# Strassen's scheme for two row tile pairs of the merge gates, with later x loads and transposes

## The chip, the cores and the metric
The kernel runs on one core of one Trainium2 chip. The metric is device time in microseconds (us) of one execution, the median of several runs. TensorE (PE) multiplies, VectorE (DVE) and ScalarE (ACT) work elementwise, GpSimd (POOL) does a few elementwise steps, and SyncE (SP) issues the DMAs.

## The reference
One layer of a decoder trunk on x of 256 tokens by 2048 channels, float32. Cut to what matters here:

```
proj = rms_norm(x) @ w_in                       # 2048 x 9216; the last 4096 columns are gate_a | gate_b
y_a = multiscale_pool(u_pool) @ w_branch_a      # 1024 x 2048
y_b = hgrn2(q, f, i, g) @ w_branch_b            # 1024 x 2048
x  += (sigmoid(gate_a) * y_a + sigmoid(gate_b) * y_b) @ w_out
x  += (silu(conv3(u)_gate) * conv3(u)_val) @ w_down,   u = rms_norm(x) @ w_up
x  += sigmoid(rms_norm(x) @ w_ple_gate) * (p @ w_ple)
return rms_norm(x)
```

## The kernel before, in words
Every product is float32 made of three products of split operands. An operand t is cut into t_hi (a rounded copy) and t_lo = t - t_hi, and t times w is t_hi w_hi + t_hi w_lo + t_lo w_hi. So one row tile (128 rows of w, 128 tokens, 512 columns) costs three matmuls (L623 to L625; in the down stage `triple`, L671 to L673).

**Units and slots.** All weights come as a stream of numbered units. A unit is two row tiles of a weight by 512 columns, 512 KB. It passes through a ring of four buffers: SP loads `raw` (`rows`, L464), ACT rounds it into `w_hi` (`split_hi`, L1010), DVE subtracts to get `w_lo` (`split_lo`, L1303), and TensorE runs 12 matmuls on it (two row tiles, two token blocks, three matmuls each) and counts it in `units_done`. ACT and DVE run one list of steps, `slot(s)`, for s = 0, 1, 2 and so on. A slot first splits unit s + 3 (LEAD = 3); everything else that has its time in that slot comes behind it. Because the ring has four buffers, `split_hi(u)` waits for `units_done` of unit u - 4:

```
def split_hi(u, it=None):
    ...
    if u >= RING:
        ac.wait_ge(units_done, plus(u - RING + 1, 2 * UK, it))
```

So slot s of ACT starts when TensorE has finished unit s - 1, and slot s of DVE starts one rounding step later. SP's `slot_split(u)` waits until `w_lo` of unit u - 4 is made, and for a unit of a Strassen pair also for the sums of its weights (L457).

**Stages.** Ten chunks of 8 units are the projections (MIX = 80 units), beside which the scan and the pooling run. The merge stage follows: for each of four column chunks n (512 columns), 8 units of gate a, 8 of gate b, 4 of w_branch_a (y_a) and 4 of w_branch_b (y_b), 24 units in all, each product in one of two halves of the PSUM tensor `main` by turns. ACT applies the sigmoid when a gate is done (`store`), DVE multiplies y_a and y_b with the sigmoids (L1665) and adds the two into `m_tok` (L1670); TensorE transposes `m_tok` into the PSUM tensor `aux` behind the first unit of the next chunk (side job `mT`, L789), and ACT and DVE split the result for w_out (L1213, L1673). Then come w_out (32 units), w_up (176 units), w_down (172 units), and the last gate. `merge_slot(n, k)` is the slot after which chunk n's product k (gate a, gate b, y_a, y_b) is complete.

**The Strassen pairs of the down stage.** Two adjacent column chunks share the activations. At five places of each half (`SEVEN_AT`) a 2 by 2 block problem (two row tiles, two token blocks, two column chunks) is done with 7 products in place of 8. DVE makes four sums of the raw weights (`weight_diffs`, L1548 to L1552) in the slot two ahead, ACT rounds them (L1165), DVE makes their low parts (L1576), and POOL and DVE make sums of the activations (L1842, L1559 to L1571). TensorE runs 3 of the 7 products with the two units and the other 4 in two halves behind the next two units (`down_sums`). Four of the products collect in banks of their own. At the end of each half ACT copies the first (L1184) and DVE combines them (`combine`, L1590), from slot `down_slot(2p) - 4` on, five units after the last pair's first unit; TensorE waits for the fifth combining step, which is in slot `down_slot(2p) - 2`, at the start of the next half, ten units after that pair's first unit.

`x_tok`, the token major x that w_out's result is added to, is loaded in four pieces of 512 KB during the projections (`X_TOK_AT`, L498).

Of the kernel before, what the change touches and what calls it, by code (L numbers as in the profile page):

```python
# [36 lines left out]
P = 128  # L37
# [60 lines left out]
def merge_slot(n, k):  # L98

    return MIX + n * 2 * (UK + UB) + (UK, 2 * UK, 2 * UK + UB, 2 * (UK + UB))[k]  # L100
# [21 lines left out]
SEVENS = [down_unit(p, i) for p in range(2) for i in SEVEN_AT[p]]  # L122
SEVEN = {u: q for q, u in enumerate(SEVENS)}
SUMS_AT = {max(u - 4, DOWN + UK): q for q, u in enumerate(SEVENS)}
N_SEVEN = [len(SEVEN_AT[0]), len(SEVENS)]

# [9 lines left out]
def chunk_end(c):  # L136
# [17 lines left out]
X_TOK_AT = [20, 24, 28, 32]  # L154
# [15 lines left out]
    + [(merge_slot(n, 3) + 1, f"mT{n}") for n in range(NQ)]  # L170
# [21 lines left out]
X2_AT = {down_slot(n) + 2: n for n in range(NQ)}  # L192
COMBINE_AT = [down_slot(2 * p) - 4 for p in range(2)]
# [18 lines left out]
def build(nc, x, x_t, p_t, vecs, convs, w_in, pool_mix_w, w_branch_a, w_branch_b, w_out, w_up, w_down,  # L212
          w_ple_gate, w_ple, ln_final_w, ident_c, levels_c, counts_c, out):
    with ExitStack() as ctx:
# [21 lines left out]
        sb("fill", [P, FILL])  # L236
        x_tok = sb("x_tok", [P, TB, D])
# [124 lines left out]
        x2_turned, copied, combined = map(sem, ("x2_turned", "copied", "combined"))  # L362

# [23 lines left out]
        def main_acc(c, tb, width=NCOL):  # L387
            return main[:, c % 2, tb, 0:width]

# [60 lines left out]
        def _(sp):  # L450
# [43 lines left out]
            for u in range(UK, MIX):  # L494
                rows(u, w_in_v, 2 * (u % UK), PROJ[u // UK])
                if u in X_TOK_AT:
                    n = X_TOK_AT.index(u)
                    sp.dma_start(x_tok[:, :, cols(n)], x_v[:, :, cols(n)]).then_inc(tok_in, 16)  # L498
                if u == 14:
                    sp.dma_start(convT[:], convs).then_inc(conv_in, 16)  # L500
                    sp.dma_start(levels[:], levels_c).then_inc(late_in, 16)
                    sp.dma_start(counts[:], counts_c).then_inc(late_in, 16)
                    sp.dma_start(mixw[:].rearrange("p g a n -> p (g a) n"),
                                 pool_mix_w[0].rearrange("g (a p) n -> p (g a) n", p=P)).then_inc(late_in, 16)
            u = MIX
            for n in range(NQ):
                for w, k, col in ((w_in_v, UK, COL_GA), (w_in_v, UK, COL_GB), (w_a_v, UB, 0), (w_b_v, UB, 0)):
# [53 lines left out]
        def _(pe):  # L561
            def main_released(c):

                if c < 8:
                    g, k = c // 4, c % 4
                    pe.wait_ge((tok_ready, tok_ready, v_ready, g_ready)[k], (4 * g + 2, 4 * g + 4, 2 * g + 2, 2 * g + 2)[k])
                elif c < C_MIX:
                    pe.wait_ge(tok_ready, 8 + 2 * (c - 7))
                elif c < C_WOUT:
                    n, k = (c - C_MIX) // 4, (c - C_MIX) % 4  # L570
                    pe.wait_ge(gates_ready if k < 2 else gated, 4 * n + 2 * (k % 2 + 1))
                elif c < C_UP:
                    pe.wait_ge(x_new, 2 * (c - C_WOUT + 1))
                elif c < C_DOWN:
                    pe.wait_ge(z_read, c - C_UP + 2)
                elif c < C_GATE:
                    pe.wait_ge(combined, 13)
                else:
                    pe.wait_ge((sig_ready, emb_ready)[(c - C_GATE) % 2], 2 * ((c - C_GATE) // 2 + 1))

            def aux_released(name):

                kind, g = name.rstrip("0123456789."), name.split(".")[0][-1:]
                g = int(g) if g.isdigit() else 0
                if kind == "ms":
                    pe.wait_ge(ms_ready, 1)
                elif kind == "qT":
                    pe.wait_ge(qT_ready, g + 1)
                elif kind == "fT":
                    pe.wait_ge(sig_f, 2 * (g + 1))  # L590
                elif kind == "diag":
                    pe.wait_ge(sc_ready, 8 * g + 1)
                elif kind == "prod" and name[-1] != "8":
                    pe.wait_ge(sc_ready, 8 * g + 1 + int(name[-1]))
                elif kind == "prod":
                    pe.wait_ge(scX_ready, g + 1)
                elif kind == "pv":
                    pe.wait_ge(o_ready, g + 1)
                elif kind == "obT":
                    pe.wait_ge(obT_ready, 4 * (g + 1))  # L600
                elif kind == "uT":
                    pe.wait_ge(uT_ready, g + 1)
                elif kind == "mix":
                    pe.wait_ge(yaT_ready, 4 * (g + 1))
                elif kind == "mT":
                    pe.wait_ge(mT_ready, g + 1)
# [53 lines left out]
            def chunk_unit(u, c, i, n, hi, lo, k, **more):  # L660
# [3 lines left out]
                for name in AUX_AT.get(u, ()):  # L664
                    side(name)
                if u in X2_AT:
                    turn_x2(X2_AT[u])

# [15 lines left out]
            def sum_tile(t):  # L684
                return w_sums_hi[:, t, :], w_sums_lo[:, t, :]
# [11 lines left out]
            def down_seven(u, p, i, a):  # L697
# [12 lines left out]
                else:  # L710
                    pe.wait_ge(a_sums_ready, q + 1)
# [3 lines left out]
            def down_sums(u, p, i, half):  # L715
# [4 lines left out]
                if half == 0:  # L720
                    triple(product(p, 1), *act_sum(q, 3), *sum_tile(0), start=first, stop=end)
                    mm = triple(product(p, 3), *act_sum(q, 1), *sum_tile(1), start=first, stop=end)
                else:
                    triple(product(p, 2), *act_sum(q, 0), *sum_tile(2), start=first, stop=end)
                    mm = triple(down_acc(2 * p, 1), *act_block(2 * i + 1, 1), *sum_tile(3), start=False, stop=False)
# [57 lines left out]
            def transposes(name, src, n=4):  # L783

                dst = aux_blocks(name)
                for b in range(n):
                    for tb in range(TB):
                        at = in_time(tb) if name[:2] in ("mT", "uT") else slice(tb * P, (tb + 1) * P)
# [57 lines left out]
            def side(name):  # L846
# [25 lines left out]
                elif name[:2] == "mT":  # L872
                    pe.wait_ge(m_ready, int(name[2]) + 1)
                    transposes(name, tok_block(m_tok))
# [32 lines left out]
            for n in range(NQ):  # L907
                for k, (hi, lo, nu) in enumerate(((xT_hi, xT_lo, UK), (xT_hi, xT_lo, UK),
                                                  (yaT_hi, yaT_lo, UB), (obT_hi, obT_lo, UB))):
                    for i in range(nu):  # L910
                        if n == 0 and i == 0 and k >= 2:

                            pe.wait_ge((yaT_ready, obT_ready)[k - 2], 8)
                        chunk_unit(u, C_MIX + 4 * n + k, i, nu, hi, lo, 2 * i)
# [21 lines left out]
            for p in range(2):  # L936
                if p:
                    pe.wait_ge(combined, 5)
# [59 lines left out]
        def _(ac):  # L998
# [153 lines left out]
            def sums_hi(q, part):  # L1152

                if part == 0:
                    ac.wait_ge(a_summed, q + 1)
                    if q > 1:
                        ac.wait_ge(w_sums_done, 2 * (q - 1))
                    ac.activation(a_sums_hi[:, q % 2].rearrange("p k t -> p (k t)"), a_sums[:].rearrange("p k t -> p (k t)"),
                                  ACT.Copy).then_inc(a_sums_hi_ready, 1)
                else:  # L1160
# [4 lines left out]
                    ac.activation(w_sums_hi[:, 2 * half:2 * half + 2, :], w_sums[:, 2 * half:2 * half + 2, :],  # L1165
                                  ACT.Copy).then_inc(w_sums_hi_ready, 1)

            def slot(s):
# [9 lines left out]
                if s in SEVEN:  # L1178
                    sums_hi(SEVEN[s], 2)
                for p in range(2):  # L1180
# [21 lines left out]
                for n in range(NQ):  # L1202
                    if s == merge_slot(n, 0):
                        if n:
                            ac.wait_ge(m_ready, n)
                        else:
                            ac.wait_ge(dT_ready, 2)
                        store(C_MIX + 4 * n, lambda tb: sig_a[:, tb, :], 0, gates_ready, ACT.Sigmoid)
                    if s == merge_slot(n, 1):
                        store(C_MIX + 4 * n + 1, lambda tb: sig_b[:, tb, :], 0, gates_ready, ACT.Sigmoid)  # L1210
                    if s == merge_slot(n, 3) + 2:
                        aux_arrived(ac, f"mT{n}")
                        ac.activation(mT_hi[:, 4 * n:4 * n + 4, :], aux_blocks(f"mT{n}"), ACT.Copy).then_inc(mT_hi_ready, 1)  # L1213
# [78 lines left out]
        def _(dve):  # L1292
# [274 lines left out]
            def sums_lo(q, part):  # L1567
# [5 lines left out]
                else:  # L1573
                    half = slice(2 * (part - 1), 2 * part)
                    dve.wait_ge(w_sums_hi_ready, 2 * q + part)
                    dve.tensor_tensor(w_sums_lo[:, half, :], w_sums[:, half, :], w_sums_hi[:, half, :].bitcast(F32),  # L1576
                                      ALU.subtract).then_inc(w_sums_ready, 1)

            combines = [0]

            def combine(p, part):
# [10 lines left out]
                if part == 0:  # L1592
                    dve.wait_ge(copied, p + 1)
# [15 lines left out]
            def slot(s):  # L1609
# [11 lines left out]
                for k in range(2):  # L1621
                    if s - k in SEVEN:
                        sums_lo(SEVEN[s - k], k + 1)
                for p in range(2):
# [34 lines left out]
                for n in range(NQ):  # L1659
# [6 lines left out]
                    if s == merge_slot(n, 3):  # L1666
                        dve.wait_ge(gated, 4 * n + 4)
                        if n:
                            aux_arrived(dve, f"mT{n - 1}")
                        dve.tensor_tensor(m_tok[:], sig_a[:], sig_b[:], ALU.add).then_inc(m_ready, 1)  # L1670
                    if s == merge_slot(n, 3) + 2:
                        dve.wait_ge(mT_hi_ready, n + 1)
                        dve.tensor_tensor(mT_lo[:, 4 * n:4 * n + 4, :], aux_blocks(f"mT{n}"),  # L1673
# [118 lines left out]
        def _(pool):  # L1792
# [42 lines left out]
            def join_act(u, q):  # L1835

                k = u - DOWN - 2 * UD * (u >= DOWN + 2 * UD)
                if q == 0:
                    pool.wait_ge(aT_ready, NUP)
                else:  # L1840
                    pool.wait_ge(a_sums_ready, q)
                pool.tensor_tensor(a_sums[:], aT_hi[:, k:k + 2, :].bitcast(F32), aT_lo[:, k:k + 2, :].bitcast(F32),  # L1842
# [6 lines left out]

            root(1)  # L1850
# [3 lines left out]
            for q, u in enumerate(SEVENS):  # L1854
                join_act(u, q)
# [51 lines left out]
```

## Time and profile before

| | us |
|---|---|
| median of 3 runs | 1436.45 (1436.11 to 1436.77) |
| the profiled execution: own time | 1436.71 |
| the profiled execution: span from first to last instruction | 1434.9 |
| TensorE busy in the span | 1424.6 (99%) |
| DVE busy | 990.4 (69%) |
| ACT busy | 761.5 (53%) |
| POOL busy | 168.8 (12%) |
| mean granted TensorE clock | 0.999 |

A matmul's entry lasts longer than its turn on the engine, since matmuls are pipelined; what one costs is the distance between two starts.

### The profile page before, as it was taken

How to read it: one execution, taken by the hardware profiler on the slowest of the kernel's cores; microseconds unless marked ns; L12 is line 12 of the kernel's file. 1: busy time of each engine (PE TensorE's matmuls, PEld its weight loads, DVE VectorE, ACT ScalarE, POOL GpSimd, SP SyncE). 2: the span in 40 equal slices, each digit the busy share in tenths (PEclk: the TensorE clock that was granted, in tenths of full speed). 3: DMA queues.
4: the chain of work that ended last, by engine and by line, in shares of the span. 5: the costliest groups of instructions: out<-in, count | busy, mean ns of one | idle time of the engine just before them, and what ended most of it. 6: DMA issues, size and time to landing. Idle time of an engine off the chain costs nothing.

```text
span 1434.9 us, 19704 instructions
## 1 busy us (share of the span) xinstructions
PE 1424.6 (99%) x7112; PEld 1211.5 (84%) x7112; DVE 990.4 (69%) x1220; ACT 761.5 (53%) x920; POOL 168.8 (12%) x113
## 2 busy tenths in 40 slices
PE   9999999999999999999999999999999999999997
PEld 7888888888888888888888888888888888888886
DVE  7676777845455455566777777777777888887755
ACT  7555655544444444555555555555555555555644
POOL 0044144100000000000101101111011100000000
PEclk9999999999999999999999999999999999999999
DMA  9765555556666655465666566565665665556653
GB/s 326 224 205 161 163 174 164 155 183 191 191 190 191 191 191 189 157 207 183 188 191 191 179 198 185 182 200 178 192 192 175 204 205 192 175 192 220 228 199 123
DMA packets 190876, 273.47 MB, mean 191 GB/s; under 512 B 11744, under 2 KB 103136, under 8 KB 190688
## 3 DMA queue, kind: packets, MB, share of 16 engines
q1 hardware_dynamic: 190384, 272.30, 59.9%
q8 instruction: 38, 0.62, 0.2%
q10 hardware_dynamic: 432, 0.37, 0.1%
q14 instruction: 22, 0.18, 0.0%
HBM read 270.53 MB, written 2.10 MB: 190 GB/s over the span
## 4 chain that ended last, share of the span: by engine, by line
PE 98%; DVE 1%; issue 0%; DMA 0%; ACT 0%; ACTq 0%; POOLq 0%; POOL 0%; DVEq 0%
PE main L623 15%; PE main L624 15%; PE main L625 15%; PE aux L748 11%; PE main L748 11%; PE aux L757 6%; PE main L757 6%; PE aux L671 3%; PE aux L672 3%; PE aux L673 3%; PE main L671 3%; PE main L673 3%; PE main L672 2%; PE aux L819 1%; PE aux L789 1%; PE aux L842 0%
## 5 line engine op out<-in xcount | busy, mean ns | idle before, releaser
L1303 DVE TENSOR_TENSOR w_lo<-raw,w_hi 128x1024 fp32r<-128x1024 f32 (+1 forms) x490 | 604.3, 1243 | 387.6 <-ACT w_hi L1010 387.1
L1010 ACT ACTIVATE w_hi<-raw 128x1024 fp32r<-128x1024 f32 (+1 forms) x490 | 515.0, 1052 | 547.2 <-PE main L625 282.6
L623 PE MATMUL main<-w_hi,xT 128*128 128x512 f32 x702 | 276.7, 394 | 0.3 <-DVE w_lo L1730 0.3
L625 PE MATMUL main<-w_hi,xT 128*128 128x512 f32 x702 | 273.6, 390 | 0.0
L624 PE MATMUL main<-w_lo,xT 128*128 128x512 f32 x702 | 273.5, 390 | 0.0
L748 PE MATMUL aux<-xT,w_hi 128*128 128x512 f32 x704 | 169.8, 391 | 0.0
L748 PE MATMUL main<-xT,w_hi 128*128 128x512 f32 x672 | 163.0, 391 | 0.0
L623 PEld LDWEIGHTS main<-w_hi,xT 128*128 128x128 f32 x702 | 132.0, 188 | 27.3 <-DVE xT L1330 1.0
L625 PEld LDWEIGHTS main<-w_hi,xT 128*128 128x128 f32 x702 | 131.8, 188 | 27.4
L624 PEld LDWEIGHTS main<-w_lo,xT 128*128 128x128 f32 x702 | 132.0, 188 | 26.1
L748 PEld LDWEIGHTS aux<-xT,w_hi 128*128 128x128 f32 x704 | 129.4, 188 | 25.2 <-issue 0.3
L748 PEld LDWEIGHTS main<-xT,w_hi 128*128 128x128 f32 x672 | 123.3, 188 | 23.5
L1848 POOL TENSOR_TENSOR act<-cv 128x512 f32<-128x512 f32 (+1 forms) x22 | 71.9, 3266 | 418.9 <-DVE cv L1527 418.9
L757 PEld LDWEIGHTS aux<-xT,w_lo 128*128 128x128 f32 x704 | 90.3, 191 | 3.4
L757 PE MATMUL aux<-xT,w_lo 128*128 128x256 f32 x704 | 91.3, 283 | 0.0
L757 PEld LDWEIGHTS main<-xT,w_lo 128*128 128x128 f32 x672 | 86.4, 191 | 3.4
L757 PE MATMUL main<-xT,w_lo 128*128 128x256 f32 x672 | 87.5, 283 | 0.0
L1527 DVE SCALAR_TENSOR_TENSOR cv<-z,convT,cv 128x255 f32<-128x255 f32 (+1 forms) x172 | 71.7, 479 | 3.0
L1795 POOL TENSOR_TENSOR st<-st,minus_half 128x2 f32<-128x2 f32 (+1 forms) x5 | 3.2, 642 | 530.6 <-DVE st L1361 399.6
L1141 ACT ACTIVATE cv<-z,convT 128x256 f32<-128x256 f32 x86 | 44.8, 591 | 24.1 <-DVE z L1518 24.1
L671 PE MATMUL aux<-w_hi,aT_hi 128*128 128x512 f32 x142 | 55.6, 391 | 0.0
L671 PE MATMUL main<-w_hi,aT_hi 128*128 128x512 f32 x142 | 55.4, 390 | 0.0
(270 smaller groups left out, 1737.3 us busy)
## 6 DMA issues: line engine op xcount, KB each, us to landing
raw<-in_w_up SPq DMA_DIRECT2D x336, 256.0 KB
raw<-in_w_in SPq DMA_DIRECT2D x136, 512.0 KB
raw<-in_w_down SPq DMA_DIRECT2D x84, 512.0 KB
raw<-in_w_out SPq DMA_DIRECT2D x32, 512.0 KB
raw<-in_w_ple_gate SPq DMA_DIRECT2D x32, 512.0 KB
raw<-in_w_branch_a SPq DMA_DIRECT2D x16, 512.0 KB
raw<-in_w_branch_b SPq DMA_DIRECT2D x16, 512.0 KB
raw<-in_w_in SPq DMA_DIRECT2D x15, 256.0 KB, 5.6
```

What stands on the lines that cost most here:

```text
L623: pe.matmul(acc, th, wh, start=first, stop=False)
L624: pe.matmul(acc, th, wl, start=False, stop=False)
L625: return pe.matmul(acc, tl, wh, start=False, stop=end)
L671: pe.matmul(acc, th, wh, start=start, stop=False)
L672: pe.matmul(acc, th, wl, start=False, stop=False)
L673: return pe.matmul(acc, tl, wh, start=False, stop=stop)
L748: mm = pe.matmul(up_acc(j, b), w_hi[:, u % RING, a, b * P:(b + 1) * P], xT[:, k, :, :].rearrange("p h t -> p (h t)"), start=(k == 0), stop ...
L757: mm = pe.matmul(up_acc(j, b)[:, 0:SEQ], w_lo[:, u % RING, a, b * P:(b + 1) * P], xT[:, k, 0, :], start=False, stop=False)
L1010: ac.activation(w_hi[:, u % RING, :, 0:w], raw[:, u % RING, :, 0:w], ACT.Copy).then_inc(hi_full, 1)
L1303: dve.tensor_tensor(w_lo[:, u % RING, :, 0:w], raw[:, u % RING, :, 0:w], w_hi[:, u % RING, :, 0:w].bitcast(F32), ALU.subtract).then_inc(lo ...
L1527: last_op = dve.scalar_tensor_tensor(out=cv[:, b, d:SEQ], in0=z[:, b, 0:SEQ - d], scalar=convT[:, tap, f0(f)], in1=cv[:, b, d:SEQ], op0=AL ...
L1848: pool.tensor_tensor(act[:, 0:nf, :], cv[:, 0:nf, :], cv[:, nf:2 * nf, :], ALU.mult).then_inc(prod_u, 1)
```

## The change
For merge chunks 1 to 3 the units of gate a and gate b alternate, one row tile pair i of both at a time (`gate_unit(n, i, a)`), and both gates add up in `main`, a in half 0 and b in half 1. At i = 2 and i = 5 (`GATES_AT`) the pair is done with 7 products in place of 8. Four of these collect in `aux`. y_a and y_b of every chunk now use `aux` as well. ACT copies one of the products, DVE combines the four (`combine_gates`) and adds the combined terms to both gates (`sum_gates`), and ACT applies the sigmoids in place. The activation sums are made once, during chunk 0, and serve all three chunks. Their weight sums lie in new tensors at the address of `x_tok`; `x_tok` is therefore loaded later, during y_a and y_b of chunk 3, behind a wait of SP for the last weight sums. The transposes of `m_tok` move from behind the first to behind the third unit of the next chunk, always into `aux[0]`. In the down stage only counters change.

```diff
 def merge_slot(n, k):
-    return MIX + n * 2 * (UK + UB) + (UK, 2 * UK, 2 * UK + UB, 2 * (UK + UB))[k]
+    return MIX + n * 2 * (UK + UB) + (2 * UK - 1 if n and k == 0 else UK, 2 * UK, 2 * UK + UB, 2 * (UK + UB))[k]
+def gate_unit(n, i, a=0):
+    return MIX + n * 2 * (UK + UB) + 2 * i + a
...
+GATES_AT = (2, 5)
+N_GATES = len(GATES_AT) * (NQ - 1)
+SEVENS = [gate_unit(n, i) for n in range(1, NQ) for i in GATES_AT] + [down_unit(p, i) for p in range(2) for i in SEVEN_AT[p]]
...
-X_TOK_AT = [20, 24, 28, 32]
+X_TOK_AT = [gate_unit(NQ - 1, UK) + 2 * n + 1 for n in range(NQ)]
...
+MT_AT = {merge_slot(n, 3) + 2: n for n in range(NQ)}
+GATES_COMBINE_AT = [gate_unit(n, GATES_AT[-1]) + 5 for n in range(NQ)]
...
 # SP, units of the merge stage
+                        if u in X_TOK_AT:
+                            j = X_TOK_AT.index(u)
+
+                            sp.wait_ge(w_sums_done, 2 * N_GATES)
+                            sp.dma_start(x_tok[:, :, cols(j)], x_v[:, :, cols(j)]).then_inc(tok_in, 16)
...
 # TensorE, merge stage
+                else:
+                    if n == 1:
+                        pe.wait_ge(gates_ready, 4)
+                    else:
+                        pe.wait_ge(gate_sums, 4 * (n - 1))
+                    for i in range(UK):
+                        for a in range(2):
+                            if i in GATES_AT:
+                                gate_seven(u, n, i, a)
+                            else:
+                                gate_plain(u, i, a)
+                            if u - 2 - a in SEVEN:
+                                gate_weight_sums(u - 2 - a, n, i - 1, a)
+                            if u in MT_AT:
+                                turn_m(MT_AT[u])
+                            u += 1
+                    pe.wait_ge(combined, 4 * n)
+                for k, (hi, lo) in enumerate(((yaT_hi, yaT_lo), (obT_hi, obT_lo))):
+                    for i in range(UB):
+                        unit(u, C_MIX + 4 * n + 2 + k, i, UB, hi, lo, 2 * i)
                         u += 1
...
 # ACT, slot(s)
+                for n in range(1, NQ):
+                    if s == GATES_COMBINE_AT[n] - 1:
+                        done = 2 * len(GATES_AT) * n
+                        ac.wait_ge(w_sums_done, done)
+                        ac.wait_ge(w_sums_ready, done)
+                        ac.activation(w_sums[:, 0, :], gate_product(0), ACT.Copy).then_inc(copied, 1)
+                    for k, sig in enumerate((sig_a, sig_b)):
+                        if s == merge_slot(n, k) + 2:
+                            for tb in range(TB):
+                                ac.wait_ge(gate_sums, 4 * (n - 1) + 2 * k + tb + 1)
+                                ac.activation(sig[:, tb, :], sig[:, tb, :], ACT.Sigmoid,
+                                              scale=rstd[:, 0, tb:tb + 1]).then_inc(gates_ready, 1)
...
 # DVE; add_up is one tensor_tensor add that counts in combined
+            def combine_gates(n, part):
+                p5, p6, p7 = (gate_product(k) for k in range(1, 4))
+                t = [w_sums[:, k, :] for k in range(4)]
+                if part == 0:
+                    dve.wait_ge(copied, n)
+                    dve.wait_ge(m_ready, n)
+                    add_up(sig_b[:, 1, :], p6, t[0])
+                    dve.wait_ge(combined, combines[0])
+                    add_up(t[1], p5, sig_b[:, 1, :])
+                if part == 1:
+                    add_up(t[2], p7, sig_b[:, 1, :])
+                    dve.wait_ge(combined, combines[0])
+                    add_up(t[3], p5, t[2])
+            def sum_gates(n, k):
+                t = [w_sums[:, j, :] for j in range(4)]
+                chunk_done(dve, C_MIX + 4 * n + k)
+                dve.wait_ge(combined, combines[0])
+                for tb in range(TB):
+                    dve.tensor_tensor((sig_a, sig_b)[k][:, tb, :], main[:, k, tb, :], t[2 * tb + k], ALU.add).then_inc(gate_sums, 1)
...
 # DVE, slot(s), behind split_lo(s + LEAD)
+                for n in range(1, NQ):
+                    if GATES_COMBINE_AT[n] <= s < GATES_COMBINE_AT[n] + 2:
+                        combine_gates(n, s - GATES_COMBINE_AT[n])
+                    for k in range(2):
+                        if s == merge_slot(n, k) + 1:
+                            sum_gates(n, k)
```

## Rows read from the trace of the kernel before

**Rows 1.** The page, busy time: engine, busy us (share of span) x instructions.
```profile
PE 1424.6 (99%) x7112; PEld 1211.5 (84%) x7112; DVE 990.4 (69%) x1220; ACT 761.5 (53%) x920; POOL 168.8 (12%) x113
```
**Rows 2.** The page, the chain that ended last, by engine.
```profile
PE 98%; DVE 1%; issue 0%; DMA 0%; ACT 0%; ACTq 0%; POOLq 0%; POOL 0%; DVEq 0%
```
**Rows 3.** Waits of TensorE, whole run: who waited for whom, total, times, longest.
```profile
PE main L671 <- DVE a_sums_lo L1571: 0.3, 1, 0.3
```
**Rows 4.** Stretches (merge; down's second half): bounds, length, PE, PEld, DVE, ACT, POOL busy, PEclk.
```profile
383.00:450.00 67.00, 67.00 (x302) 55.59 (x301) 34.08 (x30) 29.40 (x30) 0.00 (x0) 1.00 0.63 190
1210.00:1325.00 115.00, 115.00 (x516) 95.18 (x515) 95.59 (x114) 62.37 (x76) 6.30 (x4) 1.00 0.59 196
```
**Rows 5.** Timeline, end of merge chunk 1: start, duration, instruction, [idle before].
```profile
393.72 0.39 PE L623 MATMUL main<-w_hi,xT 128*128 128x512 f32 x1
...
393.98 1.06 ACT L1010 ACTIVATE w_hi<-raw 128x1024 fp32r<-128x1024 f32 x1 [1.66 <-PE main L625]
...
395.08 1.23 DVE L1303 TENSOR_TENSOR w_lo<-raw,w_hi 128x1024 fp32r<-128x1024 f32 x1 [1.49 <-ACT w_hi L1010]
...
396.22 1.28 DVE L1665 TENSOR_TENSOR sig_b<-main,sig_b 128x512 f32<-128x512 f32 x2
...
396.44 0.39 PE L623 MATMUL main<-w_hi,xT 128*128 128x512 f32 x1
...
397.53 1.22 DVE L1670 TENSOR_TENSOR m_tok<-sig_a,sig_b 128x1024 f32<-128x1024 f32 x1
...
399.17 1.03 PE L789 MATMUL aux<-ident,m_tok 128*128 128x128 f32 x8
```
**Rows 6.** The down stage's combining adds: ns min/median/max, first and last start.
```profile
L1590 DVE TENSOR_TENSOR w_sums<-aux,w_sums x4: 681/683/685, 1203.8 to 1208.3; 128x512 f32<-128x512 f32 x4
```
**Rows 7.** Timelines, down stage, last Strassen pair: weight sums, SP's load, ACT's next splits.
```profile
1301.57 0.69 DVE L1550 TENSOR_TENSOR w_sums<-raw,w_sums 128x512 f32<-128x512 f32 x1
1302.30 0.69 DVE L1552 TENSOR_TENSOR w_sums<-raw,w_sums 128x512 f32<-128x512 f32 x1
...
1303.07 6.86 SPq L464 DMA_DIRECT2D raw<-in_w_down  x5
...
1307.22 1.06 ACT L1010 ACTIVATE w_hi<-raw 128x1024 fp32r<-128x1024 f32 x1 [1.92 <-DMA raw<-in_w_down]
...
1308.84 1.06 ACT L1010 ACTIVATE w_hi<-raw 128x1024 fp32r<-128x1024 f32 x1 [0.56 <-DMA raw<-in_w_down]
...
1310.13 1.06 ACT L1010 ACTIVATE w_hi<-raw 128x1024 fp32r<-128x1024 f32 x1 [0.23 <-DMA raw<-in_w_down]
```
**Rows 8.** Timeline, down stage, the one place where TensorE waits for DVE.
```profile
1125.14 0.69 DVE L1571 TENSOR_TENSOR a_sums_lo<-a_sums,a_sums_hi 128x512 fp32r<-128x512 f32 x1
...
1125.98 0.47 PE L671 MATMUL main<-w_hi,a_sums_hi 128*128 128x512 f32 x1 [0.31 <-DVE a_sums_lo L1571]
...
1126.29 0.40 PE L672 MATMUL main<-w_lo,a_sums_hi 128*128 128x512 f32 x1
```
**Rows 9.** Stretches behind the last matmul, columns as in Rows 4.
```profile
1426.80:1431.50 4.70, 0.03 (x1) 0.00 (x0) 2.93 (x10) 2.70 (x7) 0.55 (x1) 1.00 0.60 240
1431.60:1434.90 3.30, 0.00 (x0) 0.00 (x0) 0.00 (x0) 0.00 (x0) 0.00 (x0) 0.50 0.74 284
```
**Rows 10.** The loads of x_tok by line: issue, and time from issue to landing.
```profile
L498 SPq DMA_DIRECT2D x_tok<-in_x x4: 456/456/456, 45.6 to 84.5; - x4
...
DMA to landing us min/median/max: 4.6/4.7/5.1
```
**Rows 11.** First weight sum by line (ns min/median/max), and one beside POOL's join.
```profile
L1548 DVE TENSOR_TENSOR w_sums<-raw x10: 1212/2312/2318, 1121.4 to 1300.3; 128x1024 f32<-128x1024 f32 x10
...
1267.69 1.67 POOL L1842 TENSOR_TENSOR a_sums<-aT_hi,aT_lo 128x512 f32<-128x512 f32 x1 [14.45 <-DVE a_sums_lo L1571]
...
1268.14 2.31 DVE L1548 TENSOR_TENSOR w_sums<-raw 128x1024 f32<-128x1024 f32 x1
```

More of the change, by code:

```diff
@@ L236, in build @@
         sb("fill", [P, FILL])
+        gating = ExitStack()
+        gate_sums_hi = sb("gate_sums_hi", [P, 4, NCOL], F32R, gating)
+        gate_sums_lo = sb("gate_sums_lo", [P, 4, NCOL], F32R, gating)
+        gating.close()
         x_tok = sb("x_tok", [P, TB, D])
@@ L387, in main_acc, with gate_product, m_blocks, sums_parts @@
         def main_acc(c, tb, width=NCOL):
+            if C_MIX <= c < C_WOUT and (c - C_MIX) % 4 >= 2:
+                return aux[:, (c - C_MIX) % 2, tb * NCOL:tb * NCOL + width]
             return main[:, c % 2, tb, 0:width]
+        def gate_product(k):
+            return aux[:, 1 - k % 2, (k // 2) * NCOL:(k // 2 + 1) * NCOL]
+        def m_blocks():
+            return aux[:, 0, :].rearrange("p (b t) -> p b t", t=SEQ)
+        def sums_parts(q):
+            if q < N_GATES:
+                return gate_sums_hi, gate_sums_lo
+            return w_sums_hi, w_sums_lo
         def down_acc(n, tb):
@@ L569, in main_released @@
                 elif c < C_WOUT:
[L570 to L571 removed]
+                    pe.wait_ge(gate_sums, 4 * (NQ - 1))
                 elif c < C_UP:
@@ L576, in main_released @@
                 elif c < C_GATE:
-                    pe.wait_ge(combined, 13)
+                    pe.wait_ge(combined, COMBINED0 + 13)
                 else:
@@ L665, in chunk_unit, with turn_m @@
                     side(name)
+                if u in MT_AT:
+                    turn_m(MT_AT[u])
                 if u in X2_AT:
                     turn_x2(X2_AT[u])
+            def turn_m(n):
+                pe.wait_ge(m_ready, n + 1)
+                for b in range(4):
+                    for tb in range(TB):
+                        mm = pe.transpose(m_blocks()[:, b, in_time(tb)], tok_block(m_tok)(b, tb), ident[:])
+                mm.then_inc(m_turned, 1)
             def triple(acc, th, tl, wh, wl, start, stop):
@@ L720, in down_sums @@
                 if half == 0:
-                    triple(product(p, 1), *act_sum(q, 3), *sum_tile(0), start=first, stop=end)
-                    mm = triple(product(p, 3), *act_sum(q, 1), *sum_tile(1), start=first, stop=end)
-                else:
-                    triple(product(p, 2), *act_sum(q, 0), *sum_tile(2), start=first, stop=end)
-                    mm = triple(down_acc(2 * p, 1), *act_block(2 * i + 1, 1), *sum_tile(3), start=False, stop=False)
+                    triple(product(p, 1), *act_sum(q, 3), *sum_tile(q, 0), start=first, stop=end)
@@ new lines, in down_sums, with x_block_t @@
+                    mm = triple(product(p, 3), *act_sum(q, 1), *sum_tile(q, 1), start=first, stop=end)
+                else:
+                    triple(product(p, 2), *act_sum(q, 0), *sum_tile(q, 2), start=first, stop=end)
+                    mm = triple(down_acc(2 * p, 1), *act_block(2 * i + 1, 1), *sum_tile(q, 3), start=False, stop=False)
+                mm.then_inc(w_sums_done, 1)
+            def x_block_t(k, tb):
+                return xT_hi[:, k, tb * P:(tb + 1) * P], xT_lo[:, k, tb * P:(tb + 1) * P]
@@ new lines, in gate_plain, with gate_seven @@
+            def gate_plain(u, i, a):
+                pe.wait_ge(lo_full, u + 1)
+                for t in range(2):
+                    for tb in range(TB):
+                        mm = triple(main[:, a, tb, :], *x_block_t(2 * i + t, tb), *ring_tile(u, t),
+                                    start=i == 0 and t == 0, stop=i == UK - 1 and t == 1)
+                mm.then_inc(units_done, 1)
+            def gate_seven(u, n, i, a):
+                q = SEVEN[u - a]
+                first, end = i == GATES_AT[0], i == GATES_AT[-1]
+                pe.wait_ge(lo_full, u + 1)
+                if a == 0:
+                    if first:
+                        pe.wait_ge(gated, 4 * n)
+                    triple(gate_product(0), *x_block_t(2 * i, 0), *ring_tile(u, 0), start=first, stop=end)
+                    mm = triple(main[:, 0, 0, :], *x_block_t(2 * i + 1, 0), *ring_tile(u, 1), start=False, stop=False)
+                else:
+                    pe.wait_ge(a_sums_ready, q % 2 + 1)
+                    mm = triple(main[:, 1, 0, :], *act_sum(q, 2), *ring_tile(u, 1), start=False, stop=False)
+                mm.then_inc(units_done, 1)
@@ new lines, in gate_weight_sums @@
+            def gate_weight_sums(u, n, i, half):
+                q = SEVEN[u]
+                first, end = i == GATES_AT[0], i == GATES_AT[-1]
+                pe.wait_ge(w_sums_ready, 2 * q + half + 1)
+                if half == 0:
+                    if first:
+                        pe.wait_ge(mT_ready, n)
+                    triple(gate_product(1), *act_sum(q, 3), *sum_tile(q, 0), start=first, stop=end)
+                    mm = triple(gate_product(3), *act_sum(q, 1), *sum_tile(q, 1), start=first, stop=end)
+                else:
+                    triple(gate_product(2), *act_sum(q, 0), *sum_tile(q, 2), start=first, stop=end)
+                    mm = triple(main[:, 0, 1, :], *x_block_t(2 * i + 1, 1), *sum_tile(q, 3), start=False, stop=False)
@@ L937, in _ @@
                 if p:
-                    pe.wait_ge(combined, 5)
+                    pe.wait_ge(combined, COMBINED0 + 5)
                 else:
@@ L1575, in sums_lo, with add_up @@
                     dve.wait_ge(w_sums_hi_ready, 2 * q + part)
-                    dve.tensor_tensor(w_sums_lo[:, half, :], w_sums[:, half, :], w_sums_hi[:, half, :].bitcast(F32),
+                    hi, lo = sums_parts(q)
+                    dve.tensor_tensor(lo[:, half, :], w_sums[:, half, :], hi[:, half, :].bitcast(F32),
                                       ALU.subtract).then_inc(w_sums_ready, 1)
             combines = [0]
+            def add_up(out, a, b):
+                combines[0] += 1
+                return dve.tensor_tensor(out, a, b, ALU.add).then_inc(combined, 1)
+            def combine_gates(n, part):
[15 more added lines that the diff above has]
+                dve.wait_ge(combined, combines[0])
+                for tb in range(TB):
+                    dve.tensor_tensor((sig_a, sig_b)[k][:, tb, :], main[:, k, tb, :], t[2 * tb + k], ALU.add).then_inc(gate_sums, 1)
             def combine(p, part):
@@ L1848, in product @@
                 pool.tensor_tensor(act[:, 0:nf, :], cv[:, 0:nf, :], cv[:, nf:2 * nf, :], ALU.mult).then_inc(prod_u, 1)
+            for f in range(2):
+                join_parts(f, 0)
             root(1)
@@ L1853, in _ @@
                 product(1, 2, it)
-            for q, u in enumerate(SEVENS):
-                join_act(u, q)
+            for f, u in enumerate(ACT_SUMS[2:], 2):
+                join_parts(f, u)
             root(2)
```

94 lines of the change are left out of this document (51 added, 43 removed).

## The prediction
> **What bounds the kernel now.** I read the page's busy times first: TensorE is busy 99% of the span [rows 1]. Then the chain that ended last, to see whether that is work on the path: 98% of it is TensorE [rows 2]. Then TensorE's waits: once the stream runs, it waits for another engine only once, for 0.3 us in the down stage [rows 3]. The stretches say the same of the two stages that matter: in the merge stage TensorE is busy for all of 67 us, with DVE at half its time, and in the down stage's second half for all of 115 us, with DVE at 83% [rows 4]. So any matmul taken out is worth its full turn, if nothing makes TensorE wait; and any wait put in costs its full length, since TensorE has nothing behind it to catch up with. The sum below is therefore matmuls removed against new gaps.
>
> **The matmuls removed.** A unit of 12 matmuls runs from 393.72 to 396.44 [rows 5]: 2.72 us, 0.227 us each. A pair done with 7 products saves one product of 3 matmuls. There are 2 pairs in each of 3 chunks: 6 x 3 x 0.227 = 4.1 us off.
>
> **The new wait in front of y_a.** This is the term that decides. TensorE finishes a chunk's 16 gate units (0 to 15 of the chunk) and then waits for `combined` to reach 4n, that is for all four adds of `combine_gates`. Parts 0 and 1 stand in DVE's slots 15 and 16. Slot 16 starts with the split of unit 19, whose buffer is free only when unit 15 is done. So the last two adds can't begin before TensorE has stopped. The delay from the boundary of a unit is in the merge stage's own rows: boundary 393.72, rounding starts 393.98, `w_lo` 395.08, the next DVE step 396.22, which is 2.50 us behind the boundary [rows 5]. Then come two adds of 0.68 us on PSUM [rows 6], the second waiting for the first; a dependent pair starts 0.73 us apart [rows 7]. The second ends at 2.50 + 0.73 + 0.68 = 3.91 us. From the end of the DVE step to TensorE's first matmul is 1125.98 - 1125.83 = 0.15 us, and its second matmul comes 0.31 in place of 0.23 us later [rows 8]. Together 3.9 + 0.15 + 0.08 = 4.1 us of gap per chunk. Nothing covers it: y_a's units are already split, and the instruction stream behind the wait is y_a itself. Part 0 isn't late: slot 15 ends 2.50 + 1.41 = 3.9 us behind unit 14's boundary, 1.2 us into slot 16's own 2.5. Chunks 1 and 2: 8.2 us.
>
> **Chunk 3 has SP's wait as well.** SP issues the load of unit 17, then waits until the last weight sums are used, then issues an x_tok piece, and only then the load of unit 18. Call h the time when the second half of the second pair ends; units 14 and 15 follow, so TensorE stops at h + 5.44. Before, the load of unit 18 would have gone out as soon as unit 14 was split. Now SP is let go at h + 0.26 (the lag from boundary to rounding in rows 5). From such a release to the start of the rounding took 1307.22 - 1303.07 = 4.15 us for the first 512 KB, 1.62 for the next and 1.29 for the third [rows 7]; x_tok's pieces landed 4.7 us after issue [rows 10]. With x_tok first, unit 18 can be rounded at h + 0.26 + 4.15 + 1.62 = h + 6.0 and unit 19 at h + 7.3. Then: `w_lo` of 18 starts 1.10 later, h + 7.1, part 0 starts at h + 8.3 and ends 1.41 later at h + 9.7; `w_lo` of 19 follows, part 1 starts at h + 10.8, ends at h + 12.2, and TensorE starts at h + 12.3. Less 5.44, with the slow second start: a gap of 6.9 us. If the x_tok piece took none of unit 18's time, unit 18 would be there at h + 4.4 and the gap would be 5.3; if SP's hold were hidden altogether, 4.1; if each piece took one step of 1.6 more, 8.5. I take 6.9. Later pieces have the gap itself to land in, and w_out's first add is 16 units off.
>
> **TensorE's clock.** Behind the last matmul the granted clock stays at the upper level for 4.7 us and is at half in the next stretch, 2.4 to 1.2 GHz [rows 9]. A gap of 4.1 us is shorter than that silence, one of 6.9 us longer. So I let the clock fall once, in chunk 3. No row shows it rising again. Every matmul at half clock costs 0.227 us more; if it stays low as long as it took to fall, 4.7 us, the loss is 2.35 us. Bounds: 0 (it rises as work starts) to 4.7 (twice as long). I take 2.3.
>
> The Trainium skill, "TensorE: Matmul & The Clock Gate", section "Why this matters for your kernels", speaks against this change: it asks that matmul bursts have no gaps between them, because gaps put the array back to the half clock. By that rule as it stands all three gaps would count, the 4.1 us ones too; the one silence in rows 9 can't refute it for a gap of 4.1. That is the second rival.
>
> **What I cost at nothing.** (1) The pairs' elementwise work: weight sums (1.22 us where POOL is idle, 2.31 beside its join [rows 11]), two of 0.69, and two splits of the sums. In the down stage five such pairs, six units apart like these, ran in 115 us without a gap, with POOL's join beside them and the activation sums made anew each time [rows 4]; here the sums are made once and POOL is idle. The first pair is the tight one, since slot 0 has the gating and `m_tok` and slot 3 the split of the transposes. Counted along DVE from the chunk's start: `m_tok` ends at 397.53 + 1.22 - 393.72 = 5.0 [rows 5], a split of 1.1, a half one of 0.6 that must wait for its rounding until 6.4, the weight sums 2.7 to 3.8, a split of 1.1, and then ACT's roundings of unit 6, of the first two sums and of the transposes (each 1.0 to 1.1, from 8.4 on) set the pace: low part of the transposes from 11.6, split of unit 7 from 13.0, low part of the sums done at 15.4. TensorE wants it behind unit 6: units 0 to 3 and 6 at 2.72, units 4 and 5 at 1.36 and 0.68, and the transposes at 1.03 [rows 5] make 16.7. Cover 1 us; without it up to 1 us a pair, 6 in all; a gain is excluded, as TensorE can't be more than busy. (2) The longer hold of `raw` by the weight sums: the first late unit is rounded at about 14, its low part and then the second half of the sums come at 18 to 20, wanted at 20.7. (3) The transposes of `m_tok`: the same eight per chunk, now two units later; the aux buffer is wanted by the pair's products only behind unit 6, 7.5 us later, and splitting takes 2.5. w_out wants the last one at its unit 6. (4) The second gate's sigmoids are now on SBUF and in slots 17 and 18; y_a's gating is in slot 20. (5) The old loads of x_tok were hidden, so moving them returns 0. (6) Chunk 0 waits for both branches before y_a and not one before each; both are done some 7 units before.
>
> **Sum.** -4.1 + 8.2 + 6.9 + 2.3 = +13.3 us. The profiled execution took 1436.71 us (span 1434.9 and 1.8 around it); 1450.0 would be its time, and 1449.8 against the median, 0.26 lower.
>
> **The rivals.**
> (a) The gaps are there and the clock holds through all three. For it: two of them are shorter than the only silence that rows 9 show, and the third exceeds it by 2 us. -4.1 + 15.1 = +11.0: 1447.5. 20%.
> (b) The clock falls at each gap: two more times 2.3. +17.9: 1454.4. For it the rule above; against it rows 9, with a silence above 4.1. 16%.
> (c) SP's hold in chunk 3 is hidden, three equal gaps of 4.1, the clock unmoved: -4.1 + 12.3 = +8.2: 1444.7. Against it: the 4.15 us of latency start only at h. 10%.
> (d) The other side, faster: the combining adds get done before TensorE asks. It decides at the place of part 1: if it ran 4.1 us earlier, that is before unit 15's boundary, the gaps vanish and 4.1 us stay as gain: 1432.3. Against it is the order in slot 16, where the split of unit 19 stands ahead, and that split can't precede unit 15's end; I see no way round. 4%.
> (e) As forecast but with the pairs' weight sums late too, +13.3 and up to 6: 1453. 5%.
> The forecast itself holds 45%.
>
> **The numbers.** 1449.8. (a) to (c) and (e) end between 1444.7 and 1454.4, so 1444.0 to 1454.5 leaves out (d) and tails. A measurement of this kernel tells 0.2% (2.9 us) from no change. Only (d) is faster, 4%; within 0.2% would take gaps of 7 us in all, 2%; slower 94%.
>
> **What would show it.** In the profile after, TensorE's waits list shows y_a's first matmul (the L623 line on yaT_hi) waiting for DVE's add, three times, 4 us and 4 us and about 7 us; DVE's rows show in each gap a rounding, a `w_lo` and two adds in a row. TensorE has 18 fewer matmuls, and 2.04 us for a pair's two units. In chunk 3 ACT waits for the DMA of unit 18. PEclk is below 1 only in the stretch behind chunk 3's gap. If PE is dense at y_a's start, (d) holds and I am wrong in the main term; if the gaps are there but their sum differs, the clock or SP's hold was mis-sized.

## The result, and the profile after

The changed kernel took 1456.37 us (median of 4 runs, 1454.23 to 1456.53) against 1436.61 before: ratio 1.0133, 95% interval 1.0121 to 1.0146. It is 19.8 us slower, where +13.3 was forecast and 1454.5 was the end of the range. The profiled execution took 1456.45 us, with a span of 1454.7 us and a mean granted clock of 0.991.

I read it in the order of the prediction. In the changed kernel's lines L715 to L717 are a gate unit's three matmuls, L657 to L659 those of y_a, L494 the loads of `raw`, L1114 their rounding, L1416 the low part, L1698 the combining adds and L546 the loads of x_tok. First the busy times of the page, against [rows 1]:

```profile
PE 1429.4 (98%) x7094; PEld 1212.8 (83%) x7094; DVE 1033.4 (71%) x1284; ACT 773.0 (53%) x937; POOL 171.5 (12%) x115
```

TensorE has 18 matmuls fewer (7112 to 7094), as worked out, and yet is busy 4.8 us longer. That can't be more work; matmuls must have become slower somewhere. Then TensorE's waits, against [rows 3] (who waited for whom: total, times, longest):

```profile
PE aux L657 <- DVE w_sums L1698: 15.0, 3, 7.4
PE main L968 <- DVE junk L1871: 1.1, 1, 1.1
PE main L677 <- DVE w_hi L1873: 0.4, 1, 0.4
PE main L715 <- DVE a_sums_lo L1684: 0.3, 1, 0.3
```

The first line is new. L657 into `aux` is y_a's first matmul, L1698 is the combining add; three waits. The next is the first of the three gaps in the timeline (start, duration, instruction, idle before), against [rows 5]:

```profile
370.15 0.39 PE L717 MATMUL main<-w_hi,xT 128*128 128x512 f32 x1
370.15 0.68 DVE L1698 TENSOR_TENSOR sig_b<-aux,w_sums 128x512 f32<-128x512 f32 x1
...
370.63 1.06 ACT L1114 ACTIVATE w_hi<-raw 128x1024 fp32r<-128x1024 f32 x1 [1.66 <-PE main L717]
370.87 0.69 DVE L1698 TENSOR_TENSOR w_sums<-aux,sig_b 128x512 f32<-128x512 f32 x1
371.72 1.22 DVE L1416 TENSOR_TENSOR w_lo<-raw,w_hi 128x1024 fp32r<-128x1024 f32 x1 [0.16 <-ACT w_hi L1114]
372.86 0.68 DVE L1698 TENSOR_TENSOR w_sums<-aux,sig_b 128x512 f32<-128x512 f32 x1
373.58 0.69 DVE L1698 TENSOR_TENSOR w_sums<-aux,w_sums 128x512 f32<-128x512 f32 x1
374.33 0.80 PE L657 MATMUL aux<-w_hi,yaT_hi 128*128 128x512 f32 x1 [3.79 <-DVE w_sums L1698]
...
374.92 0.63 PE L658 MATMUL aux<-w_lo,yaT_hi 128*128 128x512 f32 x1
375.35 0.63 PE L659 MATMUL aux<-w_hi,yaT_lo 128*128 128x512 f32 x1
```

Read it downward: the last gate matmul at 370.15, then rounding, split, two adds in a row, and y_a at 374.33. A start would have been due at 370.38, so 3.95 us are lost. The second thing to see is on the last two lines: 0.43 us between starts where a matmul took 0.23 [rows 5]. The stretches around it give the clock (bounds, length, PE, PEld, DVE, ACT, POOL busy, PEclk, DMA share, GB/s), columns as in [rows 4]:

```profile
364.00:370.20 6.20, 6.20 (x29) 5.07 (x27) 2.42 (x3) 2.55 (x3) 0.00 (x0) 1.00 0.66 222
370.30:373.00 2.70, 0.23 (x2) 0.00 (x0) 2.50 (x4) 1.06 (x1) 0.00 (x0) 1.00 0.53 180
373.20:379.80 6.60, 5.47 (x13) 4.31 (x14) 2.33 (x4) 0.00 (x0) 0.00 (x0) 0.50 0.25 80
380.00:386.00 6.00, 6.00 (x28) 4.93 (x27) 3.65 (x4) 4.96 (x7) 0.00 (x0) 1.00 0.33 87
...
516.60:526.60 10.00, 5.51 (x13) 4.37 (x14) 5.65 (x8) 0.67 (x1) 0.00 (x0) 0.50 0.80 306
```

The clock went from the upper to the lower level 2.8 us into the gap, at 373.1, and stayed there until 380.0. From 374.33 to 380.01 thirteen matmuls were started; at 0.227 they would have taken 2.95 us, so 2.73 are lost. This happened behind each of the three gaps: chunk 2's gap has the same length (441.69 to 445.87), and the line below is its stretch; the last stretch above is chunk 3's. Fourteen slow matmuls lose 2.81 us in chunk 2, thirteen 2.74 in chunk 3.

```profile
444.90:451.50 6.60, 5.63 (x13) 4.47 (x14) 2.17 (x4) 0.04 (x1) 0.00 (x0) 0.50 0.25 80
```

In chunk 3 SP's wait comes on top. Its only wait at L546 is for the pair's last half, the first line below; the others are the timeline:

```profile
SPq L546 <- PE main L717: 7.4, 1, 7.4
...
508.25 0.37 SPq L546 DMA_DIRECT2D x_tok<-in_x  x1
508.67 1.00 SPq L494 DMA_DIRECT2D raw<-in_w_branch_a  x2
...
514.93 1.06 ACT L1114 ACTIVATE w_hi<-raw 128x1024 fp32r<-128x1024 f32 x1 [6.08 <-DMA raw<-in_w_branch_a]
516.02 1.23 DVE L1416 TENSOR_TENSOR w_lo<-raw,w_hi 128x1024 fp32r<-128x1024 f32 x1 [6.75 <-ACT w_hi L1114]
...
518.49 1.22 DVE L1416 TENSOR_TENSOR w_lo<-raw,w_hi 128x1024 fp32r<-128x1024 f32 x1
519.62 0.68 DVE L1698 TENSOR_TENSOR w_sums<-aux,sig_b 128x512 f32<-128x512 f32 x1
...
521.09 0.80 PE L657 MATMUL aux<-w_hi,yaT_hi 128*128 128x512 f32 x1 [7.43 <-DVE w_sums L1698]
```

SP gets free at 508.25, x_tok goes out first, and unit 18 can be rounded only at 514.93. TensorE's last gate matmul was at 513.27; 7.6 us are lost.

The balance of the profiled execution: -4.1 (18 matmuls), +3.95 +3.95 +7.6 (gaps), +2.73 +2.81 +2.74 (half clock) = +19.7 us, against 1456.45 - 1436.71 = +19.7 measured. The terms make up the whole difference.

### The profile page after: what moved, and what is told of

The parts are those of the page before. It is cut to its first block, busy times and chain, and to the rows that moved or that the text cites. A ratio compares the mean times of both kernels' runs of the same rounds, so it can differ in the third digit from the quotient of the medians.

```text
span 1454.7 us, 19780 instructions
## 1 busy us (share of the span) xinstructions
PE 1429.4 (98%) x7094; PEld 1212.8 (83%) x7094; DVE 1033.4 (71%) x1284; ACT 773.0 (53%) x937; POOL 171.5 (12%) x115
## 4 chain that ended last, share of the span: by engine, by line
PE 97%; DVE 1%; DMA 1%; issue 0%; ACT 0%; ACTq 0%; POOLq 0%; POOL 0%; SPq 0%; DVEq 0%
PE aux L835 11%; PE main L835 11%; PE main L657 10%; PE main L658 10%; PE main L659 10%; PE aux L844 6%; PE main L844 6%; PE main L715 5%; PE main L717 5%; PE main L716 5%; PE aux L716 3%; PE aux L717 3%; PE aux L715 3%; PE aux L657 2%; PE aux L659 2%; PE aux L658 2%
## 5 line engine op out<-in xcount | busy, mean ns | idle before, releaser
L1416 DVE TENSOR_TENSOR w_lo<-raw,w_hi 128x1024 fp32r<-128x1024 f32 (+1 forms) x484 | 596.6, 1244 | 356.7 <-ACT w_hi L1114 356.2
L1114 ACT ACTIVATE w_hi<-raw 128x1024 fp32r<-128x1024 f32 (+1 forms) x484 | 508.1, 1052 | 539.1 <-PE main L659 158.5
L657 PE MATMUL main<-w_hi,xT 128*128 128x512 f32 x510 | 201.4, 395 | 0.3 <-DVE w_lo L1878 0.3
L658 PE MATMUL main<-w_lo,xT 128*128 128x512 f32 x510 | 198.6, 389 | 0.0
L659 PE MATMUL main<-w_hi,xT 128*128 128x512 f32 x510 | 198.5, 389 | 0.0
L657 PEld LDWEIGHTS main<-w_hi,xT 128*128 128x128 f32 x510 | 95.8, 188 | 20.1 <-DVE xT L1443 1.1
L659 PEld LDWEIGHTS main<-w_hi,xT 128*128 128x128 f32 x510 | 95.7, 188 | 20.0
L658 PEld LDWEIGHTS main<-w_lo,xT 128*128 128x128 f32 x510 | 95.8, 188 | 18.8
L715 PE MATMUL main<-w_hi,xT 128*128 128x512 f32 x150 | 58.6, 391 | 0.0
L717 PE MATMUL main<-w_hi,xT 128*128 128x512 f32 x150 | 58.4, 389 | 0.0
L716 PE MATMUL main<-w_lo,xT 128*128 128x512 f32 x150 | 58.4, 389 | 0.0
```

The costliest lines, as they stand in the source:

```text
L657: pe.matmul(acc, th, wh, start=first, stop=False)
L658: pe.matmul(acc, th, wl, start=False, stop=False)
L659: return pe.matmul(acc, tl, wh, start=False, stop=end)
L715: pe.matmul(acc, th, wh, start=start, stop=False)
L716: pe.matmul(acc, th, wl, start=False, stop=False)
L717: return pe.matmul(acc, tl, wh, start=False, stop=stop)
```

## The experiments

Seven kernels; the first four were timed beside 1436.88 us for the kernel before, the last three beside 1436.99.

**1. The second pair one step earlier.**
```diff
-GATES_AT = (2, 5)
+GATES_AT = (2, 4)
```


> Theory: the whole loss is TensorE's wait for the combining adds, because they stand in the slots of units 15 and 16, and the clock that falls behind it. With the second pair at i = 4 in place of 5 the adds stand in slots 13 and 14, and the last ends 3.9 us behind unit 13's end, 1.5 us before TensorE asks at unit 15's end. No gap in chunks 1 to 3, also none from SP's hold (it ends two units earlier, and unit 18's rounding is no longer in front of the adds), no fall of the clock; what stays is 18 matmuls less: 4.1 us below the kernel before, 1432.4 us. Rival 1: the interleaved gates, the late x_tok loads or the y products in aux cost something of their own: then it is above 1433. Rival 2: the pairs themselves starve TensorE (weight sums late, pairs now four units apart): waits for w_sums' low parts inside the gate units, up to 1 us a pair, 1432.4 to 1438.

Measured: 1432.82 us (8 runs, 1432.35 to 1433.49), ratio 0.9971, interval 0.9961 to 0.9982: 4.06 us faster than before, where 4.1 was worked out. The timeline at the place of chunk 1's former gap:

```profile
367.59 0.68 DVE L1698 TENSOR_TENSOR w_sums<-aux,sig_b 128x512 f32<-128x512 f32 x1
368.31 0.69 DVE L1698 TENSOR_TENSOR w_sums<-aux,w_sums 128x512 f32<-128x512 f32 x1
...
370.31 0.39 PE L717 MATMUL main<-w_hi,xT 128*128 128x512 f32 x1
370.53 0.39 PE L657 MATMUL aux<-w_hi,yaT_hi 128*128 128x512 f32 x1
```

The last add ends at 369.0, 1.5 us before y_a is due, and y_a follows at the usual distance. In a stretch of chunks 1 and 2 TensorE is busy throughout, with DVE at 49.3 of 67 us where it was 34.1 [rows 4]:

```profile
383.00:450.00 67.00, 67.00 (x301) 55.61 (x300) 49.33 (x51) 33.28 (x35) 0.00 (x0) 1.00 0.62 196
```

So both rivals fall: the interleaving, the y products in `aux`, the later transposes, the later x_tok loads and the pairs' elementwise work are hidden, and the whole loss hangs on where the second pair stands. That one index moves the weight sums, the combining adds and SP's release together, so this run alone doesn't say which of them made the loss; experiments 4 and 6 do. This version beats both kernels, the one before by 0.3%.

**2. The combining one slot earlier.**
```diff
-GATES_COMBINE_AT = [gate_unit(n, GATES_AT[-1]) + 5 for n in range(NQ)]
+GATES_COMBINE_AT = [gate_unit(n, GATES_AT[-1]) + 4 for n in range(NQ)]
```


> The combining starts one slot earlier (slots 14 and 15), all else as in the changed kernel. ACT's copy now has to wait for the pair's last half in the slot of unit 13, so unit 17 is rounded late: gaps of 1.8 us in chunks 1 and 2 and, since unit 19's rounding is no longer in front of the adds but unit 18's still is, 4.5 us in chunk 3. Theory (place of the adds sets the gap, and the clock falls only behind long gaps): 8 us of gaps, one fall of 2.7 us, 4.1 off: +6.6, 1443 us, and no fall behind the 1.8 us gaps. Rival (any gap before y_a lets the clock fall): three falls, +12, 1448.5.

Measured: 1443.54 us (ratio 1.0048, interval 1.0032 to 1.0063), against 1443 expected. The waits:

```profile
PE aux L657 <- DVE w_sums L1698: 7.7, 3, 5.2
```

The gaps were 1.4, 1.4 and 5.35 us. Behind the first two the clock stayed up, behind the third it fell. One stretch just behind the first gap, one just behind the third:

```profile
371.90:376.00 4.10, 4.10 (x18) 3.39 (x19) 2.33 (x3) 1.01 (x2) 0.00 (x0) 1.00 0.72 242
...
508.60:511.60 3.00, 3.00 (x8) 2.33 (x9) 2.22 (x3) 0.00 (x0) 0.00 (x0) 0.52 1.05 395
```

The rival is out; each of the two short gaps costs its own length and 0.1 us for a slow second start. That the time fits to 0.5 us is in part luck: gaps of 1.8, 1.8 and 4.5 us and a fall at 2.7 were expected, and the fall cost 1.7. (-4.1 + 8.15 + 0.2 + 1.7 is +6.0, and 6.7 was measured; the rest was not looked for.)

**3. Dummy matmuls in the gaps.**
```diff
+                    pe.wait_ge(copied, n)
+                    for _ in range(32 if n == NQ - 1 else 16):
+                        pe.matmul(aux[:, 1, 0:NCOL], xT_hi[:, 0, 0:P], xT[:, 0, :, :].rearrange("p h t -> p (h t)"),
+                                  start=True, stop=True)
                     pe.wait_ge(combined, 4 * n)
```


> TensorE is given dummy matmuls of 512 columns in front of its wait for the combining adds: 16 (3.6 us) in chunks 1 and 2, 32 (7.3 us) in chunk 3, into the bank of the product that ACT has already copied. The adds come when they come, so y_a starts as late as in the changed kernel (15.5 us lost in all). Theory (8.2 us of the 19.8 lost are matmuls at half clock behind silence of TensorE): the clock stays at the upper level, 1456.4 - 8.2 = 1448.2 us. Rival (the half clock follows from something else than TensorE's silence, or y_a's first matmuls are slow for another reason): 1456 us as before.

Measured: 1448.47 us, 7.9 less than the changed kernel. TensorE's wait for the adds is down from 15.0 to 0.6 us, and the clock is at the upper level all through chunk 1's place, and through those of chunks 2 and 3 as well:

```profile
PE aux L657 <- DVE w_sums L1702: 0.6, 3, 0.3
```
```profile
370.00:380.00 10.00, 9.83 (x44) 7.78 (x43) 6.75 (x9) 3.07 (x4) 0.00 (x0) 1.00 0.34 108
```

y_a begins as late as in the changed kernel, so 8 of the 20 us were lost behind the gaps and not in them, and TensorE's silence is what brought the clock down.

**4. The x_tok loads later.**
```diff
-X_TOK_AT = [gate_unit(NQ - 1, UK) + 2 * n + 1 for n in range(NQ)]
+X_TOK_AT = [gate_unit(NQ - 1, UK) + n + 4 for n in range(NQ)]
```


> The four x_tok loads are issued with units 20 to 23 of chunk 3 in place of 17, 19, 21 and 23, so that SP has loaded units 18 and 19 before it waits for the last weight sums. Theory (the third gap is longer than the others by SP's hold alone): the third gap falls from 7.6 to 4.0 us, -3.6 us, 1452.8 us, three falls of the clock stay. Rival (DMA rate with x_tok beside the weights sets it, not the hold): the gap stays near 7 us or weights come late after it, 1456 us.

Measured: 1452.49 us (1449.93 to 1453.5), with 1452.8 expected. The longest of the three waits is now 3.8 us like the other two, the clock still falls behind all three, and in the merge stage TensorE waits for nothing else, though the four loads go out with four units in a row:

```profile
PE aux L657 <- DVE w_sums L1698: 11.4, 3, 3.8
```

**5. A shorter gap in the kernel before.**
```diff
                         if n == 0 and i == 0 and k >= 2:
                             pe.wait_ge((yaT_ready, obT_ready)[k - 2], 8)
+                        if n and i == 0 and k == 2:
+                            pe.wait_ge(lo_full, u + LEAD + 1)
```


> The kernel before, with one thing added: in front of y_a in chunks 1 to 3 TensorE waits until unit 19 is split, as it would in the changed kernel, but with no combining adds behind the split. No Strassen pair, no late x_tok. The gap should be 2.6 + 0.2 = 2.8 us three times, +8.5 us if the clock stays up: 1445.3. If the clock falls behind a gap of 2.8 us as it did behind 4.0, each fall adds 2.7: 1453.5. My theory (the clock falls behind a silence of 4.0 us and not behind 1.4, between is open) leaves both; I lean to no fall, 1445.3.

Measured: 1447.84 us, +10.9 (ratio 1.0073). I had leaned to no fall; that was wrong. The gaps were 2.62 us each, and the clock fell behind the first and the third and not behind the second. Three stretches, each just behind one gap:

```profile
374.80:378.00 3.20, 3.20 (x10) 2.47 (x9) 0.00 (x0) 0.00 (x0) 0.00 (x0) 0.54 0.49 165
...
514.80:518.00 3.20, 3.20 (x10) 2.48 (x9) 0.00 (x0) 0.00 (x0) 0.00 (x0) 0.53 0.51 164
...
445.00:448.50 3.50, 3.50 (x15) 2.93 (x16) 0.00 (x0) 0.38 (x1) 0.00 (x0) 1.00 0.51 170
```

Here a fall came just after the matmuls had begun again, slowed some 8 of them and cost 1.7 us: 3 x 2.62 + 2 x 1.7 = 11.3.

**6. The full gap in the kernel before.** The two adds go into `m_tok` and are not used by the result.
```diff
+                for n in range(1, NQ):
+                    if s == merge_slot(n, 1):
+                        aux_arrived(dve, f"mT{n - 1}")
+                        dve.wait_ge(gates_ready, 4 * n + 2)
+                        dve.tensor_tensor(m_tok[:, 0, :], sig_a[:, 0, :], sig_a[:, 1, :], ALU.add).then_inc(late, 1)
+                        dve.wait_ge(late, 2 * n - 1)
+                        dve.tensor_tensor(m_tok[:, 1, :], sig_a[:, 0, :], m_tok[:, 0, :], ALU.add).then_inc(late, 1)
 ...
 # TensorE, in front of y_a of chunks 1 to 3
+                            pe.wait_ge(late, 2 * n)
```


> The kernel before, with one thing added: in DVE's slot 16 of chunks 1 to 3 two dependent adds of 512 columns into m_tok (not used by the result), and TensorE waits for the second in front of y_a. No Strassen pair, no late x_tok. Theory (place of the adds alone makes the loss): three gaps of 3.95 us, +11.9, and three falls of the clock at 2.7, +8.2: 1436.9 + 20.1 = 1457.0 us, so the loss of the changed kernel without any part of its gain. Rival (the changed kernel's gaps need its pairs, aux use or load order): gaps under 3 us or no falls, below 1449.

Measured: 1453.78 us, +16.8 (ratio 1.0118, interval 1.0101 to 1.0135), below the 1457.0 expected. The waits are the changed kernel's, without any of its pairs:

```profile
PE main L624 <- DVE m_tok L1668: 11.4, 3, 3.8
```

The clock fell three times, but only once TensorE worked again, and each fall cost 1.7 us in place of 2.7: 11.9 + 5.2 = 17.1. The gaps are the same to 0.01 us; what a fall costs is not a constant. The two stretches behind chunk 1's gap, which ended at 375.56:

```profile
375.60:376.60 1.00, 1.00 (x4) 0.82 (x5) 0.00 (x0) 0.00 (x0) 0.00 (x0) 1.00 0.91 293
376.80:380.00 3.20, 3.20 (x9) 2.43 (x9) 0.00 (x0) 0.00 (x0) 0.00 (x0) 0.50 0.09 35
```

**7. Gaps filled in part.** As experiment 3, with this line in place of 32 and 16:
```diff
+                    for _ in range(19 if n == NQ - 1 else 4):
```


> The changed kernel with fewer dummy matmuls in front of the wait for the adds: 4 (0.9 us) in chunks 1 and 2, 19 (4.3 us) in chunk 3. The adds are as late as in the changed kernel (15.5 us lost in all), but TensorE is silent for only 3.0 us in chunks 1 and 2 and 3.3 in chunk 3. Theory (the silence itself sets the clock, and a shorter one spares it): no fall, 1448.4 as with the gaps filled. Rival (it falls behind 3 us as well): 2.7 us for each fall, up to 1456.5.

Measured: 1454.08 us, 2.3 less than the changed kernel and not 8. The silences left were 3.04, 3.04 and 3.6 us; the clock fell behind all three, costing 1.7, 1.7 and 2.7:

```profile
374.80:378.00 3.20, 3.20 (x9) 2.55 (x8) 0.93 (x2) 0.00 (x0) 0.00 (x0) 0.50 0.34 117
446.40:449.60 3.20, 3.20 (x9) 2.52 (x8) 0.00 (x0) 0.37 (x1) 0.00 (x0) 0.51 0.01 4
518.10:524.70 6.60, 5.29 (x12) 4.13 (x13) 2.51 (x4) 0.00 (x0) 0.00 (x0) 0.50 0.70 256
```

My theory, that a silence of 3 us is spared, falls; the rival holds, with a smaller price for each fall.

## Why the prediction was right or wrong

- **Matmuls removed, -4.1.** Right: 18 fewer, and experiment 1 is 4.06 us faster than before.
- **The wait in front of y_a, 4.1 in chunks 1 and 2.** Right in place, chain and size: 3.95 us each. Experiment 6 makes the same gap from the adds' place alone, and experiment 1 removes it by moving them two slots up.
- **SP's wait in chunk 3, 6.9.** Right in cause (experiment 4 takes 3.6 us away), 0.7 too small. I let unit 18 be rounded 5.8 us after SP's release; it took 6.7 (508.25 to 514.93). The 5.8 came from a stretch without x_tok's loads among those of the weights; whether that is the reason was not tried.
- **The clock, one fall at 2.3.** This is the step that failed. It was three falls at 2.7 to 2.8: 8.3 in place of 2.3 accounts for 6.0 of the 6.5 us that the forecast lacks, SP's wait for most of the rest. The error was in the reading of [rows 9]: I took the 4.7 us of silence before the fall at the kernel's end as the shortest silence that lets the clock fall, when one such fall only shows that 4.7 suffices. In the changed kernel the clock fell 2.8, 2.9 and 3.0 us into the three gaps. The rule of the Trainium skill ("TensorE: Matmul & The Clock Gate", section "Why this matters for your kernels"), that gaps between bursts put the array back to its half clock, was the second rival; it had 16% and is what happened. The page says this of gaps above a certain length, which the forecast left out. The traces agree in all gaps of 3 us and more, and behind the two gaps of 1.4 us the clock stayed up. The size was low as well, though inside its bounds, and that it came near was luck: I let the clock stay low as long as it took to fall, but it took 2.8 to 3.0 us to fall and was low for 6.8.
- **What I cost at nothing.** Right throughout: TensorE has no wait in the gate units, neither in the changed kernel, whose merge stage has the three waits at y_a and no other, nor in experiment 1.
- **Rivals.** (b) at 1454.4 was nearest, 2 us short: 0.7 from SP's wait and 1.4 from the price of the falls, less 0.3 for two gaps of 3.95 in place of 4.1, and 0.2 since the kernel before took 1436.61 beside this run and not 1436.45. (a) and (c) are out. (d), faster, failed for the reason given: unit 19's split stands in front of the last two adds. The range ended at 1454.5 since it held rival (b) at its central price and none of its bounds.

## What to carry to other kernels

Where an engine is dense, a saving of 0.7 us a place is worth nothing if its result is waited for where the stream can't have made it yet. Before moving work, find for each new wait which slot the awaited step stands in and what is queued in front of it there; here one index (5 to 4) made the difference between +19.8 and -4.1 us. And count a gap of TensorE twice: its length, and the half clock behind it, unless it is short.

## What the runs showed of the hardware

By the traces of these kernels, the granted clock stayed up behind both gaps of 1.4 us, fell behind two of three of 2.6, both of 3.04, the one of 3.6, all eight of 3.95 and the ones of 5.35 and 7.6. The same 3.95 us gap cost 2.7 to 2.9 us of slow matmuls behind it in the changed kernel and in experiment 4, and 1.7 in experiment 6: in the first two the clock fell during the gap, in the last only after the matmuls had begun again. So it is in all fifteen falls at these gaps: the seven that came during a gap (three of the changed kernel, three of experiment 4, the third of experiment 7) cost 2.7 to 2.9 us, the eight that came after the matmuls had begun again cost 1.7. In chunk 1 the clock was low from 373.1 to 380.0 in the changed kernel and from 376.7 to 380.1 in experiment 6. What decides between the two was not tried. One of the changed kernel's runs took 1454.23 us with a mean clock of 0.993 where the others had 1456.3 to 1456.5 and 0.991; that is near what two such differences of 1.0 us are worth, but no profile of that run is at hand. Feeding TensorE dummy matmuls all through the gaps kept the clock up and won back 7.9 us; with silences of 3.04 and 3.6 us left it fell each time.
